# Output gates of HGRN2 heads 6 and 7: two plain products replaced by a fourteenth pair of seven quarter products

## What is computed

```python
def hgrn2_mixer(h, w_in, lb, norm_w, w_out):
    proj = h @ w_in
    fd = HG_HEADS * HG_DK
    q = jax.nn.silu(proj[..., :fd]).astype(jnp.float32)
    f = proj[..., fd:2 * fd].astype(jnp.float32)
    i = proj[..., 2 * fd:2 * fd + D_MODEL].astype(jnp.float32)
    g = proj[..., 2 * fd + D_MODEL:]
    ...
    o = hgrn2_chunkwise(split_heads(q, HG_HEADS), split_heads(k, HG_HEADS),
                        split_heads(log_f, HG_HEADS), split_heads(i, HG_HEADS))
    o = merge_heads(head_rmsnorm(o, norm_w)).astype(h.dtype) * jax.nn.silu(g)
    return o @ w_out
```

## Time and profile before

| | us |
|---|---|
| median of 3 executions | 1946.95 |
| lowest and highest | 1945.09, 1948.77 |
| span of the profiled execution | 1947.0 |

### The profile page before, as it was taken

One profiled execution on the slowest core, in us unless ns is written; L12 is line 12 of the kernel. 1 busy time (PEld: TensorE's weight loads), 2 busy tenths in 40 slices (PEclk: granted clock), 3 DMA queues, 4 the chain that ended last, 5 costly groups with the idle time before them and its releaser, 6 DMA issues. The chain is left out here.

```text
span 1947.0 us, 36169 instructions
## 1 busy us (share of the span) xinstructions
PE 1910.5 (98%) x14816; PEld 1597.2 (82%) x14816; DVE 869.2 (45%) x1177; ACT 567.5 (29%) x1210; POOL 681.2 (35%) x593
## 2 busy tenths in 40 slices
PE   9999999999999999999999999999999999999997
PEld 8778745888746888888867888745999999999996
DVE  3898687666425444444436777643100000000023
ACT  1443213455512111110036657532110211111102
POOL 6755432655314434444526777520300000000011
PEclk9999999999999999999999999999999999999999
DMA  9213750322224666631211111101967578778893
GB/s 333 88 55 152 275 193 23 103 85 69 82 65 156 214 214 214 212 127 60 103 65 67 67 67 66 56 12 62 312 212 251 197 235 274 256 266 325 333 354 144
DMA packets 82821, 313.54 MB, mean 161 GB/s; under 512 B 10121, under 2 KB 10641, under 8 KB 82529
## 3 DMA queue, kind: packets, MB, share of 16 engines
q1 hardware_dynamic: 75952, 289.73, 42.2%
q0 software_dynamic: 4464, 14.35, 2.1%
q10 hardware_dynamic: 2241, 7.14, 1.0%
HBM read 301.43 MB, written 9.75 MB: 160 GB/s over the span
## 5 line engine op out<-in xcount | busy, mean ns | idle before, releaser
L261 PE MATMUL banks<-sb_act,sb_ring 128*64 128x112 f32 (+10 forms) x5184 | 685.7, 318 | 2.8 <-DMA sb_ring<-in_w_moe_up 1.2
L261 PEld LDWEIGHTS banks<-sb_act,sb_ring 128*128 128x128 f32 (+1 forms) x5184 | 599.9, 173 | 79.6 <-issue 66.1
L261 PE MATMUL banks<-sb_x_norm,sb_ring 128*128 128x256 f32 (+3 forms) x1616 | 332.5, 406 | 2.4 <-ACT sb_ring L468 1.3
L261 PEld LDWEIGHTS banks<-sb_x_norm,sb_ring 128*128 128x128 f32 (+1 forms) x1616 | 242.9, 171 | 66.4 <-issue 29.4
L3462 DVE TENSOR_TENSOR sb_act<-sb_work,banks 128x192 f32<-128x192 f32 (+7 forms) x88 | 27.2, 309 | 485.0 <-PE banks L261 477.9
L443 POOL TENSOR_TENSOR sb_ring<-sb_ring 128x512 f32<-128x512 f32 x146 | 205.7, 1409 | 102.2 <-PE banks L261 53.0
L261 PE MATMUL banks<-sb_work,sb_ring 128*128 128x256 f32 (+2 forms) x1028 | 220.5, 409 | 2.3 <-ACT sb_ring L468 1.8
L261 PEld LDWEIGHTS banks<-sb_work,sb_ring 128*128 128x128 f32 (+1 forms) x1028 | 147.7, 168 | 53.6 <-issue 33.2
L2993 POOL DMA_INDIRECT sb_work<-first_expert_rows,sb_table x8 | 7.5, 936 | 443.5 <-DMA first_expert_rows<-sb_x_norm 441.4
L3264 ACT ACTIVATE sb_work<-banks 128x192 f32<-128x192 f32 (+7 forms) x88 | 25.8, 294 | 297.3 <-PE banks L261 295.3
L2156 ACT ACTIVATE sb_work<-banks 128x256 f32<-128x256 f32 x84 | 32.3, 384 | 216.8 <-PE banks L261 216.8
(11 more groups left out here) (503 smaller groups left out, 2456.8 us busy)
## 6 DMA issues: line engine op xcount, KB each, us to landing
sb_ring<-in_w_moe_up SPq DMA_DIRECT2D x176, 512.0 KB, 5.0
sb_ring<-in_w_moe_down SPq DMA_DIRECT2D x64, 704.0 KB, 6.0
sb_act<-in_cond_w SPq DMA_DIRECT2D x84, 512.0 KB, 4.0
sb_ring<-in_w_ffn_up SPq DMA_DIRECT2D x44, 512.0 KB, 5.5
sb_ring<-in_w_h_in SPq DMA_DIRECT2D x32, 512.0 KB, 4.1
sb_ring<-in_w_in SPq DMA_DIRECT2D x28, 512.0 KB, 6.0
sb_ring<-in_w_m_in SPq DMA_DIRECT2D x24, 512.0 KB, 4.0
sb_ring<-in_w_ffn_down SPq DMA_DIRECT2D x16, 704.0 KB, 5.7
```

Of the source, the lines that this page charges most:

```text
L261: last = m.nc.tensor.matmul(out[part], weights[:, part], act, start=start, stop=stop, skip_group_check=skip)
```

## The change

The gates of heads 6 and 7 become a fourteenth pair. Its seven quarter products are spread as `P1`, `P7`, `P6` over levels 4, 5 and 6 of head 6, `P2` and `P5` over levels 1 and 2 of head 7, and `P4`, `P3` at level 3 of head 7. Its four weight subtractions come with the products of pair 12, beside levels 0 to 3 of head 6; its copies, additions and activations follow from the same tables. `H_LAST` and all that it steered goes: the two plain products, the two takes, and the earlier place of the norm's `square` in head 6, which moves behind `keep(6, 6)`. Both early output pieces now wait for all 32 blocks. The order of the weight blocks stays the same.

```diff
--- before.py
+++ after.py
@@ -2352,10 +2352,9 @@
 H_FIRST = [("f", 0), ("q", 0), ("f", 1), ("g", 0)]
 H_PAIRS = [(("f", 2), ("q", 1)), (("v", 0), ("v", 1)), (("f", 3), ("q", 2)), (("v", 2), ("v", 3)), (("f", 4), ("q", 3)),
            (("g", 1), ("g", 2)), (("f", 5), ("q", 4)), (("v", 4), ("v", 5)), (("f", 6), ("q", 5)), (("g", 3), ("g", 4)),
-           (("f", 7), ("q", 6)), (("v", 6), ("v", 7)), (("g", 5), ("q", 7))]
-H_LAST = {(6, 5): ("g", 6), (7, 2): ("g", 7)}
-H_BLOCKS = H_FIRST + [block for pair in H_PAIRS for block in pair] + list(H_LAST.values())
-H_BESIDE = [[2, 2, 2, 1, 2, 2, 2, 1]] * 6 + [[2, 2, 2, 1, 0, 0, 0, 0], [0] * 8]
+           (("f", 7), ("q", 6)), (("v", 6), ("v", 7)), (("g", 5), ("q", 7)), (("g", 6), ("g", 7))]
+H_BLOCKS = H_FIRST + [block for pair in H_PAIRS for block in pair]
+H_BESIDE = [[2, 2, 2, 1, 2, 2, 2, 1]] * 6 + [[2, 2, 2, 1, 1, 1, 1, 0], [0, 1, 1, 2, 0, 0, 0, 0]]
 
 
 ORDERS = {"in": [IN_HOST.index(b) if b < GATE else b for b in IN_BLOCKS],
@@ -2466,12 +2465,10 @@
                 for j in range(LEVELS):
                     n = h * LEVELS + j
                     pairs.multiply(pe, H_BESIDE[h][j])
-                    if (h, j) in H_LAST:
-                        project(*H_LAST[h, j])
                     if h == HEADS - 1 and j in OUT_BESIDE:
                         b = OUT_BESIDE[j]
                         pe.wait_ge(head_out, 2 * EARLY)
-                        pe.wait_ge(m.evac, plan.done + plan.n - 1 + b)
+                        pe.wait_ge(m.evac, plan.done + plan.n)
                         out_piece(m, pe, out, heads, b, range(0, EARLY))
                     if n >= 2:
                         pe.wait_ge(level_out, n - 1)
@@ -2640,9 +2637,6 @@
                 ahead(h, 2)
                 edges(h)
                 keep(h, 2)
-                if (h, 2) in H_LAST:
-                    take(*H_LAST[h, 2])
-                    load_exponentials()
                 ahead(h, 3)
                 if 0 < h < HEADS - 1:
                     logs(h + 1)
@@ -2650,13 +2644,9 @@
                 keep(h, 4)
                 ahead(h, 4)
                 keep(h, 5)
-                if (h, 5) in H_LAST:
-                    norms[h - 1].square(m, act)
-                    take(*H_LAST[h, 5])
-                    load_exponentials()
                 ahead(h, 5)
                 keep(h, 6)
-                if h and (h, 5) not in H_LAST:
+                if h:
                     norms[h - 1].square(m, act)
                 ahead(h, 6)
                 keep(h, 7)
```

## The result

The changed kernel takes 1951.54 us (median of 11 runs, 1950.77 to 1953.92) against 1947.58 for the kernel before in the same comparison (11 runs, 1945.09 to 1949.82): a ratio of 1.0018 with a 95% interval of 1.0010 to 1.0026. A second comparison gave 1.0013 (1.0004 to 1.0022). By the two ratios it is slower by 2.5 to 3.5 us, by the medians by 4. Both intervals leave out 1, but the size is at the edge of the 0.2% that the prediction counts as no change.

A forecast was written before the change was run, and what follows sets the result against it. TensorE, busy for nearly the whole span, was taken as the bound. The first output piece 0.77 us later plus 1.40 for one slow-clock stretch gave 2.17 over 1946.95, so 1949.1 us; range 1945.0 to 1952.0.

The forecast's parts named there:

- TensorE work: Heads 6 and 7: two plain products (13.74 us) give way to seven quarter products (12.11), saving 1.63 us.
- GpSimd's fourth subtraction: Beside level 3 of head 6, a weight subtraction lengthens VectorE's chain by 0.90 us (bounds 0 and 1.86).
- Waits in head 6: TensorE waits 1.43 us ahead of level 4 and 2.38 us ahead of level 5, for VectorE's `times`.
- Norm, level 2 of head 7, gates: Waits after level 6 of head 6, at level 2 of head 7, before the first output piece: 0.55, 0.2, 2.16 us.
- 0.1 for the signal: After level 3 of head 7, VectorE's copy starts 0.1 us later; part of the 2.16 us wait for the gates.
- The clock: Heads 6 and 7: the old slow-clock loss of 1.69 us goes; one new slow stretch costs 1.40 us (0.85 to 1.69).
- the granted clock below 1.00 once in this stretch: Expected sign in the changed profile: one slow-clock stretch within heads 6 and 7.
- Sum against the profiled execution: Whole kernel: the profiled span, 1947.0, lies 0.05 from the median 1946.95, so nothing is added around it.
- DMA, SP, and what follows the heads: No load added, the later `h_out` loads cost nothing, and the difference carries unchanged from the output pieces to the end.
- no dip returns: Rival: no new slow-clock stretch in heads 6 and 7; saved work and recovered clock just eaten by waits, 1947.7 us; chance 0.30.
- The rival of a faster kernel: VectorE reaches `times` for level 5 of head 6 during quarter products, so waits are covered: at best 1941.0 us; chance 0.06.
- The one of two dips: Rival: clock falls after level 4 or 5 of head 6 and after the gates' wait: 1951.1 us or 1952.1; chance 0.18.

The follow-up runs named there:

- late_t4: The changed kernel with the fourth weight subtraction of the last pair two levels later on GpSimd: 1951.72 us, ratio to the kernel before 1.0016.
- third profile of before: The kernel before, unchanged, profiled again on chip 8: granted clock 1.00 over gate 6's product, which takes 6.87 us; values product to first output piece 27.29 us.

## Why the prediction was right, and where its terms were off

The time lies in the stated range, and the outcome, a change of about 0.2% or less, is the forecast one, on the slow side. By its steps:

- *TensorE work.* Saved 1.63 by the rows; the quarter products take 1.73 each here too. Right.
- *GpSimd's fourth subtraction.* Predicted 0.90 on VectorE's chain for the one beside level 3, measured 0.88 in the profile (11.72 less 10.84) and 0.89 by `late_t4`. The three others cost TensorE nothing, as said: its rows show no wait ahead of levels 0 to 3 of head 6. The whole length of the subtraction, 1.60, is ruled out. Right.
- *Waits in head 6.* Predicted 1.43 and 2.38, measured 1.41 and 2.39. Right.
- *Norm, level 2 of head 7, gates.* Predicted 0.55, 0.20 and 2.16; measured 0.81, 0.65 and 2.42. These three terms were too small, by 0.97 together. For the norm, the copy began 0.32 after the product (1261.13 to 1261.45), not 0.1. The profile of before had that already (0.29), in a TensorE row that the prediction does not show. For level 2, the price of 0.20 had no row behind it; the first step of the finish took 0.88 beside GpSimd's work (0.73 from 1267.20), against 0.48 in the kernel before (at 1269.40). For the gates, the step "0.1 for the signal" ahead of the copy of level 3 failed: the copy began 0.66 after the level, about 0.31 of it the signal and 0.35 because VectorE was late, for which its shorter length of 0.43 made up only a part. The prediction also says that the first output piece waits for both gates "as before". The wait in the kernel before was for 31 blocks, so for gate 6 alone; that of the changed kernel is for all 32, and a pair counts both its blocks at once. With the right sizes the walk from the values product to the output piece, 29.60 in the prediction, gives the 30.57 measured.
- *The clock.* The step that failed in kind: the 1.69 of the dip in the profile of before was booked as a gain of the change, and 1.40 for a new dip as a price. The dip was missing in the third profile of before and in both profiles of the changed kernel, where "the granted clock below 1.00 once in this stretch" was expected, and both kernels have the same mean clock over many runs. So neither entry can be booked to one of the kernels. With both left out, the prediction's own terms give -1.63 + 6.72 - 2.63 = 2.46 us, and with the waits as measured 3.42; the profiles without the dip differ by 3.28 in this stretch, and the runs show 2.96 ± 0.36 at equal clock. That the forecast of 2.17 came near is in part luck: the two entries nearly cancel.
- *Sum against the profiled execution.* The span of 1947.0 was taken to stand for the median. With the 2.0 us around it that execution took about 1949.0, above its median. The base itself was low: the median of three runs is 1946.95, that of the 71 is 1948.83. Of the 2.5 us by which the changed kernel's 1951.64 lies above the forecast of 1949.1, 1.9 are this base and 0.6 the change.
- *DMA, SP, and what follows the heads.* The output pieces and levels 4 to 7 follow unchanged: from the first to the third output piece it is 17.87 us before and 17.89 after. Waits in the mixture of experts differ between profiles of the same kernel; whether a later end of the heads changes them was not tried.

Of the rivals, "no dip returns" describes both profiles of the changed kernel, though the time is above its 1947.7: by the base, by the three terms that were too small, and by the 1.69 of the dip that it counts as won. The rival of a faster kernel failed as its "against" said: VectorE's chain held levels 4 and 5. The one of two dips was not needed: the loss came without a dip.

## What to carry to other kernels

Replacing work of a full engine by less work gains only what the waits leave: lay the new pieces where the engine already waits for another one's chain, and look at what a result shared by two blocks now has to wait for. A wait should name the last reader of the bank, not the last use of the block: here that alone was worth 2.8 us in the changed kernel and 1.65 in the version with the earlier quarter products. A slow stretch of the clock in one profile is no property of the kernel until several executions show it; compare at equal mean clock where runs list it.

## What was not expected of the hardware

The same wait of 2.06 us, in the same kernel at the same place, was followed by a stretch at half clock in two profiles (0.80 over the next 8.56 us) and not in a third (1.00), which came from another chip than the second. The execution time of one program spreads by about 10 us (1944.5 to 1954.3), and most of it goes with the mean granted clock, 1.26 us for 0.001.
